# Gated heads and the seam between two blocks: ScalarE rounds weights, TensorE filling and the final scale are moved

## What is computed

```python
def first_block(x, p, ...):
    h = rmsnorm(x, norm_mix_g)
    da_q, da_k, da_v, hg_q, hg_zf, hg_zb, hg_v, hg_g = split(h @ w_in)
    o_da = diff_attention(rotary(da_q), rotary(da_k), da_v, ...)      # 4 heads
    o_hg = hgrn2_bidirectional(hg_q, hg_zf, hg_zb, hg_v, hg_g, ...)   # 4 gated heads
    x = x + concat(o_da, o_hg) @ w_out
    x = x + conv_glu(rmsnorm(x, norm_ffn_g), ...)
    gate = sigmoid(rmsnorm(x, norm_ple_g) @ w_ple_gate)
    x = x + (p @ w_ple) * gate
    return rmsnorm(x, final_norm_g)

def second_block(x, p, ...):
    a_b, a_c, a_h, q, k, v, c_u, c_v = split(rms_norm(x, norm1_g) @ w_in)
    y_a = a_b * short_conv(a_c * a_h)
    y_b = stick_breaking_attention(rms_norm(q), rms_norm(k), v)       # 8 heads in 4 pairs
    y_c = spatial_gating(gelu(c_u), gelu(c_v), ...)
    x = x + concat(y_a, y_b, y_c) @ w_out
    x = x + square(relu(rms_norm(x, norm2_g) @ w_ff1)) @ w_ff2
    return x + sigmoid(rms_norm(x, norm3_g) @ w_ple_gate) * (p @ w_ple_proj)
```

## Time and profile before

| what | value |
|---|---|
| median of 3 runs (lowest, highest) | 3020.83 us (3018.5, 3021.81) |
| the profiled execution | 3022.66 us |
| its span, first to last instruction | 3020.8 us |
| mean granted TensorE clock | 0.986 of full speed |
| PE busy | 2932.9 us, 97% |
| DVE busy | 1597.6 us, 53% |
| POOL busy | 1038.0 us, 34% |
| ACT busy | 683.4 us, 23% |

### The profile page before, as it was taken

How to read it: one execution, slowest core, us unless ns; L and a number is a source line. 1 busy time by engine, 2 the same in 40 slices (tenths; PEclk the granted TensorE clock), 3 DMA queues, 4 the chain that set the end, 5 groups by cost and what they waited for, 6 DMA issues and landing times. The chain is left out here.

```text
span 3020.8 us, 37379 instructions
## 1 busy us (share of the span) xinstructions
PE 2932.9 (97%) x14666; PEld 2411.6 (80%) x14666; DVE 1597.6 (53%) x1747; ACT 683.4 (23%) x984; POOL 1038.0 (34%) x483
## 2 busy tenths in 40 slices
PE   6999999999999999999999999999999999999999
PEld 5778788877888888888888766678888888888887
DVE  6666565577556335515548666664543233242545
ACT  4445422222311001000133244441110000000131
POOL 2111122222434444434435211122444444444443
PEclk8999999999999999999999999999999999999999
DMA  3011110002111111111111200011211111111112
GB/s 120 21 29 32 29 35 29 28 22 77 49 49 49 49 46 45 49 48 49 59 52 49 92 22 22 22 31 40 105 42 49 49 48 46 53 42 56 58 50 81
DMA packets 43602, 145.03 MB, mean 48 GB/s; under 512 B 5728, under 2 KB 6496, under 8 KB 43232
## 3 DMA queue, kind: packets, MB, share of 16 engines
q1 hardware_dynamic: 39168, 129.35, 13.8%
q10 hardware_dynamic: 4320, 14.09, 1.2%
HBM read 132.05 MB, written 8.49 MB: 47 GB/s over the span
## 5 line engine op out<-in xcount | busy, mean ns | idle before, releaser
L549 POOL TENSOR_TENSOR w_hi<-w_raw,der 128x1024 fp32r<-128x1024 f32 (+2 forms) x236 | 425.4, 1803 | 1934.4 <-PE ps L597 1882.0
L595 PE MATMUL ps<-a_hi,w_hi 128*128 128x512 f32 x2400 | 970.1, 404 | 9.7 <-DVE a_lo L1246 8.2
L597 PE MATMUL ps<-a_hi,w_lo 128*128 128x512 f32 x2400 | 944.2, 393 | 0.0
L596 PE MATMUL ps<-a_lo,w_hi 128*128 128x512 f32 x2400 | 943.3, 393 | 0.0
L552 POOL TENSOR_TENSOR w_lo<-w_raw,w_hi 128x1024 fp32r<-128x1024 f32 (+2 forms) x238 | 608.8, 2558 | 24.3 <-ACT w_hi L1823 5.8
L595 PEld LDWEIGHTS ps<-a_hi,w_hi 128*128 128x128 f32 x2400 | 456.4, 190 | 97.7 <-issue 9.8
L597 PEld LDWEIGHTS ps<-a_hi,w_lo 128*128 128x128 f32 x2400 | 455.3, 190 | 97.7
L596 PEld LDWEIGHTS ps<-a_lo,w_hi 128*128 128x128 f32 x2400 | 457.0, 190 | 85.4
L597 PE MATMUL ps<-b_hi,w_lo 128*128 128x512 f32 x992 | 386.1, 389 | 0.0
L596 PE MATMUL ps<-b_lo,w_hi 128*128 128x512 f32 x992 | 386.1, 389 | 0.0
L595 PE MATMUL ps<-b_hi,w_hi 128*128 128x512 f32 x992 | 386.1, 389 | 0.0
(11 more groups left out here) (277 smaller groups left out, 3139.7 us busy)
## 6 DMA issues: line engine op xcount, KB each, us to landing
w_raw<-in_w_mix SPq DMA_DIRECT2D x54, 512.0 KB, 3.5
w_raw<-in_w_gu SPq DMA_DIRECT2D x44, 512.0 KB, 3.5
w_raw<-in_w_f SPq DMA_DIRECT2D x40, 512.0 KB, 3.5
w_raw<-in_w_f SPq DMA_DIRECT2D x32, 384.0 KB, 3.0
w_raw<-in_w_ple SPq DMA_DIRECT2D x20, 512.0 KB, 3.5
w_raw<-in_w_dn SPq DMA_DIRECT2D x16, 512.0 KB, 3.5
x<-in_x SPq DMA_DIRECT2D x8, 512.0 KB, 8.3
w_raw<-in_w_out SPq DMA_DIRECT2D x16, 256.0 KB, 2.6
```

The costliest lines, as they stand in the source:

```text
L549: nc.gpsimd.tensor_tensor(w_hi[:, s, 0:cols[s]], w_raw[:, s, 0:cols[s]], zero.to_broadcast([P, cols[s]]), ALU.add).then_inc(w_hi_done, 1)
L595: mm(ps[:, bank, :], wh, hi[:, k, cols], start=(k == 0), stop=False)
L596: mm(ps[:, bank, :], wh, lo[:, k, cols], start=False, stop=False)
L597: last = mm(ps[:, bank, :], wl, hi[:, k, cols], start=False, stop=(k == nk - 1))
```

## The change

Three things are joined.

- **Rounding.** For the 15 units that the gated heads 0 to 2 prepare (the five of each next head), the high part is made by ACT (`weights_high`), and POOL makes the low part alone. ACT does so at fixed places of its order: ahead of the levels, behind steps 1, 7 and 13, and ahead of the silu.
- **Filling and order of the levels.** The 48 steps are dealt into 21 parts, and slots 1, 7 and 13 get two of them (`hg_slots`): 4 steps in these three slots, 2 or 3 in the others. The turning of `hk` waits for `k_decayed` and no longer for `decayed`. DVE's taking out of a finished half moves from step 12 to step 13, behind its two multiplications.
- **The seam.** PE does 6 steps of `U_SB + 1` ahead of the thin sums and the other 2 behind them, then 4 steps of `U_SB + 2` (into bank 4) ahead of the first spread and 4 behind it. Of its second half 3 steps come ahead of the second thin sums, 3 behind them and the last 2 behind the spread. `x` is stored to `x_back` unscaled, tile by tile, in the product ahead of the seam. The final factor is kept in `rstd_f`, and DVE scales `x` with it in the second output projection, one tile ahead of each unit's addition.

```diff
+def hg_slots(h):
+    parts = filling(*hg_fill(h), 2 * LEVELS + 4 + 3)
+    slots = []
+    for i in range(2 * LEVELS + 4):
+        n = 2 if i in (1, 7, 13) else 1
+        slots.append(sum(parts[:n], []))
+        parts = parts[n:]
+    return slots
...
             def split(u0, n, cols=(T, T)):
-                def one_unit(u, s, turn, first):
-                    if not first:
+                def one_unit(u, s, turn, high_there):
+                    if not high_there:
...
+                    for u in range(n, U_OUT):
+                        one_unit(u, u % 2, u // 2, u > U_HG + 4)
...
-            split(U_DA, U_OUT)
+            split(U_DA, U_HG + 4)
...
-                slots = filling(*hg_fill(h), 2 * LEVELS + 4) if h + 1 < HEADS else out_fill()
+                slots = hg_slots(h) if h + 1 < HEADS else out_fill()
...
-                pe.wait_ge(decayed, 14 * h + 14)
+                pe.wait_ge(k_decayed, 14 * h + 14)
...
             second_unit(0, 4, KT)
+            second_unit(1, 0, 6)
             pe.wait_ge(ss_ready, Q_1 + KT)
             st_sums(fss[:, 0, :], one, 1)
             st_sums(fss[:, 1, :], one, 1, 16)
-            second_unit(1, 0, 5)
+            second_unit(1, 6, KT)
+            for k in range(4):
+                k_step(U_SB + 2, 0, k, 0, a_hi, a_lo, KT, 4)
             st_bcast(N_1, 1, 5)
-            second_unit(1, 5, KT)
+            for k in range(4, KT):
+                k_step(U_SB + 2, 0, k, 0, a_hi, a_lo, KT, 4)
...
-                gemm_half(u + 2, 0, (u + 2) % 2, a_hi, a_lo, KT)
+                at_ = 3 if p else 6
                 if p:
+                    gemm_half(u + 2, 0, (u + 2) % 2, a_hi, a_lo, KT)
...
+                else:
+                    gemm_half(u + 2, 1, (u + 2) % 2, a_hi, a_lo, KT, end=3)
                 pe.wait_ge(sq_qk, 2 * p + 2)
                 st_sums(c_buf, blk2, 2, 0, True)
                 st_sums(ss, blk2, 2, 16)
-                gemm_half(u + 2, 1, (u + 2) % 2, a_hi, a_lo, KT, end=3)
+                gemm_half(u + 2, 1, (u + 2) % 2, a_hi, a_lo, KT, first=at_ - 3, end=at_)
                 if p == 0:
-                    pe.wait_ge(xf_ready, KT)
+                    pe.wait_ge(xf_ready, 1)
                 st_bcast(N_QK + p, 2, 4, 0, True)
                 st_bcast(N_QK + p, 2, 2, 16)
-                gemm_half(u + 2, 1, (u + 2) % 2, a_hi, a_lo, KT, first=3)
+                gemm_half(u + 2, 1, (u + 2) % 2, a_hi, a_lo, KT, first=at_)
...
                         decay(l, g)
+                        if i == 2 * LEVELS - 1:
+                            leaves(slots[i - 2])
                         put(l, g)
...
-                        if i:
+                        if i and i != 2 * LEVELS - 2:
                             leaves(slots[i - 1])
...
+                def scaled(k):
+                    dve.wait_ge(x_in[k], 16 * turn)
+                    step(stt(x[:, k, :], x[:, k, :], col("final", k), rstd[:, :], ALU.mult, ALU.mult))
                 step(nc.vector.memset(ss[:, :], 0.0))
+                dve.wait_ge(xf_ready, 2)
+                scaled(0)
                 for k in range(KT):
-                    dve.wait_ge(x_in[k], 16 * turn)
                     add_to_x(u0 + k, k, bank=2 if k == 1 else 0)
+                    if k + 1 < KT:
+                        scaled(k + 1)
...
-            dve.wait_ge(st_bc, N_1 + 1)
-            for k in range(KT):
-                stt(x[:, k, :], x[:, k, :], col("final", k), banks(2), ALU.mult,
-                    ALU.mult).then_inc(xf_ready, 1)
...
-                leave_half(u + 2, 0, sv[:, :])
+                leave_half(u + 2, 0, sv[:, :], None if p else 4)
...
+            def weights_high(u):
+                act.wait_ge(w_in[u % 2], 16 * (u // 2 + 1))
+                act.wait_ge(acc_full, half_no(u - 2, 1))
+                av(w_hi[:, u % 2, :], w_raw[:, u % 2, :], ACT.Copy).then_inc(w_hi_done, 1)
...
+                if h + 1 < HEADS:
+                    weights_high(u + 5)
                 for l in range(LEVELS):
...
+                        elif h + 1 < HEADS and i in (1, 7, 13):
+                            weights_high(u + 6 + i // 6)
...
+                if h + 1 < HEADS:
+                    weights_high(u + 9)
                 act.wait_ge(acc_free, half_no(u + 4, 1))
                 av(hg[:, :], hg[:, :], ACT.Silu).then_inc(silu_done, 1)
...
                         av(to[:, 1, :], x[:, k, :], ACT.Square, scale=col("final", k)).then_inc(sq_ready, 1)
+                        act.dma_start(x_back[:, k, :], x[:, k, :]).then_inc(x_out, 16)
...
-                    for k in range(KT):
-                        act.wait_ge(xf_ready, k + 1)
-                        act.dma_start(x_back[:, k, :], x[:, k, :]).then_inc(x_out, 16)
+                    act.wait_ge(st_bc, N_1 + 1)
+                    av(rstd_f[:, :], banks(2), ACT.Copy).then_inc(xf_ready, 1)
...
                 else:
+                    act.wait_ge(xf_ready, 1)
+                    av(rstd[:, :], rstd_f[:, :], ACT.Copy).then_inc(xf_ready, 1)
                     rounded(7, 8, 2 * HEADS + 4)
```

More of the change, by code:

```diff
@@ L300, in bass_two_blocks @@
         fsq = at("fsq", (2, T), S0 + 40 * KB)
+        rstd_f = at("rstd_f", T, S0 + 60 * KB)
         fsq2 = at("fsq2", (2, T), S0 + 8 * KB)
```

## The result

The kernel after takes 2998.22 us (median of 4 runs, 2996.57 to 2999.72), the kernel before on the same chip 3019.66 us (4 runs, 3018.07 to 3021.81): a ratio of 0.9927, 95% interval 0.9911 to 0.9943, or 21.4 us less. The prediction was 2996.0 us, range 2990.5 to 3004.5. The profiled execution of after took 2998.14 us, with a span of 2996.3 at a mean clock of 0.988; that of before had 3020.8 at 0.986.

What follows compares the result with a forecast made beforehand. PE, busy 97% of the span, was taken as the bound, with only waits and half-clock stretches to gain. Levels 15.2, clock 3.2 and seam 7.2 made 25.6 us, from 3022.66 to 2997.1; forecast median 2996, range 2990.5 to 3004.5.

Steps and rivals of the forecast that it cites:

- The levels: Levels of heads 0 to 2: all 5.08 us of PE's waits per head go, 15.2 us in all.
- The free durations: Levels: with DVE's multiplications mostly unblocked, DVE has 37.6 us of work against PE's 40.5, PE fuller by 3 us.
- Clock: Tails behind the levels of heads 0 and 1: full clock, 13.73 us each, saving 3.2 us.
- Head 3: Head 3's levels: old slots, weaker wait counted as 0; clock position allowed 1.7 us either way.
- The seam: Seam: waits of 3.6 and 0.4 us go, first 32 thin sums run warm for 3.2 us; 7.2 us saved.
- The output projections: Second output projection: moved scaling of `x` costs 0, DVE needing at most 9.6 us of each 10.88 us unit.
- rival E: Second output projection: slower, DVE's operations each wait out a POOL unit; about 3048 us, chance 0.02.
- Rival A, the lost race: Step 13: POOL's low part beats DVE's `hk` multiplication, costing 1 to 2 us a head; 2999 to 3002, chance 0.15.
- Closest places: Levels: least time in hand at step 4 (0.3 us) and step 8 (0.2 to 0.4 us).
- Rival B: Clock: waits go but as many cold stretches stay; 6.4 us less gain, 3002 us, chance 0.13.
- C: Levels: POOL's low part alone still holds them back, a third of 15.2 us won; 3006 to 3008, chance 0.05.
- D: Levels: PE waits as before and only the seam's wait goes; about 3015 us, no change, chance 0.02.

Runs made afterwards that it cites:

- silenced POOL: Kernel before, with POOL treating only 16 of 1024 columns of the 15 units split during the gated heads (most weights stale); 3000.63 us, 0.9929.
- whole seam: Kernel before with both seam edits, PE's new order and the moved scaling of `x`; 3017.90 us, 0.9987.
- order alone: Kernel before with only PE's new order at the seam, the scaling of `x` left in place; 3018.55 us, 0.9989.
- scaling alone: Kernel before with only the scaling of `x` moved to the second output projection, PE's seam order unchanged; 3022.37 us, 1.0003.
- early fill: Kernel after plus a DVE fill of 512 unused columns ahead of the `hk` multiplication in step 12, heads 0 to 2; 2997.40 us, 0.9919.
- both fills: Kernel after plus a 512-column DVE fill in step 12, ahead of the `hk` multiplication (2997.40 us) or between it and that of `hqd` (2996.60 us).
- DVE's order turned round: Kernel after with DVE's order changed in the last query tile of the differential attention, heads 0 to 2; 2990.09 us, 0.9900.
- ACT alone: Kernel before with ACT making the gated heads' high parts, step dealing and waits unchanged; 3011.93 us, 0.9971.
- the order alone: Kernel before with steps dealt anew, the taking-out moved and the wait for `k_decayed`; POOL still makes both parts; 3010.67 us, 0.9970.
- ACT and the dealing: Kernel before with ACT's high parts and the new dealing, but the old `decayed` wait, taking-out and seam; 3005.93 us, 0.9949.

## Why the prediction was right, point by point

*The levels* (15.2 us). All 15.24 us of waits are gone, by ACT (3.1 a head alone), by the dealing (3.1 a head with the rest of the order) and by both together; as the silenced POOL shows, they had one cause. Not in the sum were the 0.17 us of pipeline per wait, four waits a head, 2.0 us. The stretches are 39.76 us, predicted 40.5, and that difference is about this term.

*The free durations.* DVE was to need 37.6 us and needs 38.33. The text had the third low part fall behind the last multiplication of `hk`; it starts at 456.13, well ahead of that one (459.90), so DVE is held three times and not twice, and the 3 us that PE was to be the fuller by are 1.4. The costs set at 0 held: ACT's copies are 1.04 to 1.06 us, and neither `hkd` nor `w_lo` is waited for in heads 0 to 2.

*Clock* (3.2 us). The tails take 13.08, 13.04 and 13.06 us at 1.00, one step (0.68) shorter than the warm one before: exactly that term, between these two traces. Levels and tails give 3 x 5.14 + 5.2 = 20.6, the whole of the heads' 20.7. Its size is in part luck. Four traces have heads like those of before, with a wait of 2.56 us before each turning of `hk`: half-clock stretches followed in 2, 1, 0 and 1 of their three tails (before, whole seam, order alone, scaling alone). The ten with a wait of 1.73 us or less, or none, show it in none of 30 tails. So that the wait brings the stretch is borne out; but 4 in 12 at 1.6 us each make some 1.6 us an execution (an estimate from these traces), and the forecast took the 3.2 of one.

*Head 3.* -1.3 us to the seam, inside the 1.7 allowed. One sign of being wrong did show there, 17.1 us at half clock in its levels instead of 13.7; a stretch less behind the head makes up for it.

*The seam* (7.2 us by the trace, 7.6 found). The 3.6 and the 0.4 went, the warm sums are 3.63 (predicted 3.6 to 3.7), the wait before the logits is 1.00 (1.2) and set off by the 1.19 that went. Two sizes were off and cancel. The text let the steps behind the first sums keep their cold loss; they gave back 1.5 us (4.94 for 5 steps, 4.23 for 6). Against that, the second sums with the steps behind them took 1.0 us more and the spread behind those 0.6. That DVE's scaling was only in the way of the new order, the text had not seen: it cost the move at nothing and credited the gain to TensorE's order, which alone brings 2.3.

*The output projections.* One unit in the kernel after has 10.87 us, of which DVE is idle for 2.79 before one half, and PE does not wait; the bound of 9.6 for DVE was not reached, and rival E had no ground.

*Rival A, the lost race.* The walk gave DVE 0.25 us over POOL in step 13. The 0.25 us are there (455.88 against 456.13), but in step 12, and the price was wrong for the one case tried: with POOL's recorded start 0.29 us ahead, POOL still waits for DVE, and the loss is 0.31 us and its 0.17, not 1 to 2 a head. A later `hk` wasn't tried. The Trainium skill (SBUF — State Buffer, Who interferes with whom) has the first to issue hold the shared pair for its whole instruction. The rows agree on the hold, 2.87 us for 0.69. By the recorded starts they don't agree on the first: in the kernel with the early fill the instruction with the later start ran. Whether POOL asks for the memory later than its recorded start, no run here shows.

*Closest places.* The text named steps 4 and 8. The closest is the last, with 0.06 us, and the fill ahead of `hk` shows that it has no more than that.

*Rival B* did not come (three tails at 1.00), nor did C and D. Its argument, that the wait alone does not decide, holds: 8 of 12 tails behind 2.56 us of waiting stayed at full clock.

*The sum.* 25.6 us against 24.5 in the spans: heads 2.3 more than priced, seam 0.4 more, head 3 to the seam 1.3 that was counted as 0, and on the other side 3.6 lost at the start and 1.5 behind the logits, where the sum had nothing. The medians differ by 21.4, predicted 24.8. The forecast took 1.83 us off for the profiled execution of before; it stood 3.0 above the median of four, and the two cold tails are in it. The close total is therefore partly luck: a clock term that was too large stands against 2.0 us of pipeline that were missing. The medians themselves move by some us: in the three later groups before is at 3021.0 to 3021.7. And the stretch behind the first 512-wide logits took 1291.0 to 1291.1 us in four traces of the same code (the whole seam, both fills, DVE's order turned round), with 18.4 to 19.0 us at half clock, and 1294.1 in that of after, with 24.8: those 3.1 us are the clock.

## What to carry to other kernels

When a two-input operation of VectorE takes four times its usual time, look at what GpSimd does in the same microseconds, and try both cures: give GpSimd's work to an idle engine, and deal the bottleneck's spare work to the place of the hold. Here either alone brought 12 us between the first and the last head in the traces (3.2 of them clock; 9 and 10.5 by the medians of the whole), and only the two with the small edits behind them brought 20.7. A chain that frees time on an engine nobody waits for pays nothing until the order is changed to use it, so price such parts together; and when you set a median against a trace, first compare the stretches that the change can't reach.

## What the hardware showed that I had not expected

*The hand-over between GpSimd and VectorE.* In these rows the two take turns by the instruction. At the end of head 0's levels, in six kernels (after, both fills, ACT alone, the order alone, ACT and the dealing), POOL's low part of 1024 columns ends 2.23 to 2.25 us after the VectorE multiplication it overlapped, and the next VectorE multiplication 0.54 to 0.55 us after POOL. With the fill ahead of `hk`, the multiplication that starts 0.29 us after POOL's recorded start still goes first, and POOL's part takes 3.15 us where it takes 2.35 alone. A fill without an input ran in 0.48 us beside POOL's low part: it isn't held. The Trainium skill (SBUF — State Buffer, Who interferes with whom) says that outside the two-port modes a VectorE operation with at most one input in that memory does not contend with GpSimd, and the row agrees.

*The start differs from trace to trace.* The first dense step began at 13.29 to 13.38 us in three of the profiled executions (before, ACT alone, POOL silenced), at 14.62 in one and at 15.91 to 16.30 in the other ten, for kernels whose start is the same code. The trace shows PE waiting there for VectorE's `a_lo` (8.24 to 11.08 us). That is 3 us on a change of 21. Each kernel has one trace, so whether it differs by execution or by kernel, and why, stays open.

*The clock's half stretches.* Behind the second attention's sums the same code ran 3.4 us at 1.2 GHz in some executions and 6.8 in others; behind the first 512-wide logits 6 us more at that clock went with 3.1 us more time. A wait of up to 1.73 us before the turning of `hk` was followed by a half-clock stretch in no trace, one of 2.56 in 4 heads of 12; ACT alone has the same order of PE's work as before. So a wait's price is its length plus, sometimes, a cold stretch, and one trace doesn't tell how often.
